# Two gate blocks of each mixer multiplied as a pair, with seven block products in place of eight

## The reference, cut to what matters

```
h = rms_norm(x, pre_g)
proj = h @ w_in            # 2048 x (12*1536 + 3*2048)
# attention q,k,v,z; conv u,b,c,z; retention q,k,v,z; gates g_a, g_c, g_r (2048 columns each)
merged = (sigmoid(g_a) * (o_a @ w_branch_a)
          + sigmoid(g_c) * (o_c @ w_branch_c)
          + sigmoid(g_r) * (o_r @ w_branch_r))
y = merged @ w_out
return x + rms_norm(y, post_g)
```

## Time and profile before

| what | value |
|---|---|
| median of 3 runs (lowest, highest) | 2745.49 us (2745.38, 2746.4) |
| span of the profiled execution | 2743.0 us |
| TensorE matmul busy | 2732.6 us, 12264 instructions |
| DVE busy | 1924.2 us, 2558 instructions |
| ACT busy | 1222.0 us, 1404 instructions |
| 16 DMA engines, share by the loads' queue | 57.4% |

### The profile page before, as it was taken

One profiled execution on the slowest core, in us unless ns is written; L12 is line 12 of the kernel. 1 busy time (PEld: TensorE's weight loads), 2 busy tenths in 40 slices (PEclk: granted clock), 3 DMA queues, 4 the chain that ended last, 5 costly groups with the idle time before them and its releaser, 6 DMA issues.

```text
span 2743.0 us, 30433 instructions
## 1 busy us (share of the span) xinstructions
PE 2732.6 (100%) x12264; PEld 2268.3 (83%) x12264; DVE 1924.2 (70%) x2558; ACT 1222.0 (45%) x1404; POOL 27.5 (1%) x35
## 2 busy tenths in 40 slices
PE   9999999999999999999999999999999999999998
PEld 7888888888888888888878888888888888888887
DVE  6788744777655898858567887457676558977584
ACT  6454544444443334444454545444444433434443
POOL 0000000000000000000000000000000000000000
PEclk9999999999999999999999999999999999999999
DMA  9555566565555555556575555555656565555563
GB/s 333 184 172 196 170 200 194 190 199 188 196 195 190 184 184 176 182 195 221 180 238 175 184 190 179 197 188 187 202 193 198 188 197 177 191 171 182 199 215 138
DMA packets 264732, 529.10 MB, mean 193 GB/s; under 512 B 8464, under 2 KB 8848, under 8 KB 264336
## 3 DMA queue, kind: packets, MB, share of 16 engines
q1 hardware_dynamic: 260976, 517.50, 57.4%
q10 hardware_dynamic: 2608, 4.78, 0.5%
q0 software_dynamic: 1008, 4.87, 0.5%
HBM read 522.94 MB, written 4.19 MB: 192 GB/s over the span
## 4 chain that ended last, share of the span: by engine, by line
PE 99%; DVE 0%; issue 0%; ACT 0%; DVEq 0%; POOL 0%; POOLq 0%
PE ps L651 32%; PE ps L652 32%; PE ps L653 32%; PE ps L586 0%; PE ps L606 0%; PE ps L604 0%; PE ps L603 0%; PE ps L582 0%; PE ps L567 0%; PE ps L587 0%; PE ps L581 0%; PE ps L669 0%; DVE gates L1183 0%; DVE w_trail L913 0%; DVEq L231 0%
## 5 line engine op out<-in xcount | busy, mean ns | idle before, releaser
L913 DVE TENSOR_TENSOR w_trail<-raw,w_lead 128x1024 fp32r<-128x1024 f32 x973 | 1188.7, 1225 | 763.8 <-ACT w_lead L723 754.4
L723 ACT ACTIVATE w_lead<-raw 128x1024 fp32r<-128x1024 f32 x973 | 1028.3, 1060 | 1394.1 <-PE ps L653 1387.3
L651 PE MATMUL ps<-w_lead,hT_lead 128*128 128x512 f32 x3328 | 1299.1, 390 | 0.8 <-issue 0.4
L653 PE MATMUL ps<-w_lead,hT_trail 128*128 128x512 f32 x3328 | 1295.2, 389 | 0.0
L652 PE MATMUL ps<-w_trail,hT_lead 128*128 128x512 f32 x3328 | 1295.1, 389 | 0.0
L651 PEld LDWEIGHTS ps<-w_lead,hT_lead 128*128 128x128 f32 x3328 | 625.0, 188 | 131.1 <-issue 2.2
L653 PEld LDWEIGHTS ps<-w_lead,hT_trail 128*128 128x128 f32 x3328 | 624.9, 188 | 130.0
L652 PEld LDWEIGHTS ps<-w_trail,hT_lead 128*128 128x128 f32 x3328 | 625.1, 188 | 128.4
L651 PE MATMUL ps<-w_lead,oT_lead 128*128 128x512 f32 x576 | 224.3, 389 | 0.0
L653 PE MATMUL ps<-w_lead,oT_trail 128*128 128x512 f32 x576 | 224.1, 389 | 0.0
L652 PE MATMUL ps<-w_trail,oT_lead 128*128 128x512 f32 x576 | 224.1, 389 | 0.0
(11 more groups left out here) (102 smaller groups left out, 781.7 us busy)
## 6 DMA issues: line engine op xcount, KB each, us to landing
raw<-w_in SPq DMA_DIRECT2D x381, 1024.0 KB, 5.1
raw<-w_out SPq DMA_DIRECT2D x32, 1024.0 KB, 5.0
raw<-w_branch_a SPq DMA_DIRECT2D x24, 1024.0 KB, 5.0
raw<-w_branch_c SPq DMA_DIRECT2D x24, 1024.0 KB, 5.0
raw<-w_branch_r SPq DMA_DIRECT2D x24, 1024.0 KB, 5.0
raw<-w_in SPq DMA_DIRECT2D x5, 512.0 KB, 5.0
gates<-x SPq DMA_DIRECT2D x4, 512.0 KB, 13.5
post_gain<-post_norm_g POOLq DMA_DIRECT2D x2, 1024.0 KB, 8.2
```

The source lines that it names most:

```text
L651: pe.matmul(acc, lead[:, k, tok(t)], wl, start=(k == 0), stop=False)
L653: last = pe.matmul(acc, trail[:, k, tok(t)], wl, start=False, stop=(k == BLOCKS[n][2] - 1))
L723: act.activation(w_lead[:, h % SPLIT_SLOTS, :], raw[:, i % RAW_SLOTS, part:part + HALF * COLS], ACT.Copy).then_inc(lead_ready, 1)
L913: dve.tensor_tensor(w_trail[:, s, :], raw[:, i % RAW_SLOTS, part:part + HALF * COLS], w_lead[:, s, :].bitcast(F32), ALU.subtract).then_inc ...
```

## The change

The third and fourth gate blocks of each mixer (j = 2 and 3) become a pair. On the first half of the contraction (tiles 0 to 7, taken as two chunks c = 0 and 1 of four tiles) the eight products of (token tile) x (chunk) x (block) are replaced by seven: p1, q5, p6, p7, q3, p2, q4. Four of them (`SUM_AFTER`: q5, p6, p7, q4) take a sum of two weight chunks, which DVE makes in place in `raw`; four (`FORMS`) take a combination of token-side chunks, made once a layer in `sh_lead` and `sh_trail`. The second half of the contraction is multiplied as before. A product has two units of 6 matmuls each. The pair's units (numbered 0 to 21 in what follows, with H for a unit of 12 matmuls of block n or n+1) stand in this order: p1 p1 H q5 q5 H p6 p6 H p7 p7 H q3 q3 H p2 p2 H q4 q4 H H. Before, the two blocks had 16 units of 12 matmuls.

```diff
-RAW_SLOTS = 4
+RAW_SLOTS = 5
+PAIRED_GATES = {"attention": (2,), "conv": (2,), "retention": (2,)}
...
+PRODUCTS = {"p1": ((0, 0), None), "q5": ((0, 0), (1, 0)), "p6": ((0, 0), (1, 1)), "p7": ((1, 0), (1, 1)),
+            "q3": ((1, 1), None), "p2": ((0, 1), None), "q4": ((0, 0), (0, 1))}
+PAIR_ORDER = ("p1", 0, "q5", 0, "p6", 0, "p7", 0, "q3", 1, "p2", 1, "q4", 1, 1)
+PAIR_CHUNK_ORDER = ((0, 0), (1, 0), (0, 2), (1, 1), (0, 3), (1, 2), (0, 1), (1, 3))
+
+SUM_AFTER = {"q5": "p1", "p6": "q5", "p7": "p6", "q4": "p2"}
...
+STARTS = [0]
+for _kind, _n, _at in UNITS:
+    STARTS.append(STARTS[-1] + (1 if _kind in PRODUCTS else TILES))
...
+    return next(h for h in range(HALVES) if STARTS[h] >= STARTS[FIRST_HALF[n]] + TILES * at)
...
-                out.setdefault(FIRST_HALF[first_block(mixer, g)] + at + offset, []).append((what, mixer, g))
+                out.setdefault(unit_after(first_block(mixer, g), at) + offset, []).append((what, mixer, g))
...
+FORM_STEPS = ("whole", "sums", "lead", "trail")
+FORMS_FROM = 2 * B
+
+PAIR_COPY_DUE = {UNIT_AT[kind, n, 1] + AHEAD: (kind, n) for n in PAIRS for kind in ("p1", "p6", "p7")}
+PAIR_REST_DUE = {UNIT_AT[kind, n, 1] + AHEAD + 1: (kind, n) for n in PAIRS for kind in ("p6", "p7")}
+SUM_DUE = {UNIT_AT[before, n, 1]: (kind, n) for n in PAIRS for kind, before in SUM_AFTER.items()}
...
-        post_gain = sb("post_gain", [P, D_MODEL])
-        v_sb = sb("v_sb", [P, TILES, COLS])
-        q_sb = sb("q_sb", [P, TILES, COLS])
+        vq_sb = sb("vq_sb", [P, 2, TILES, COLS])
+        v_sb, q_sb = vq_sb[:, 0], vq_sb[:, 1]
+        post_gain = vq_sb[:, :, :, :].rearrange("p a t c -> p (a t c)")
...
-        prodT = sb("prodT", [P, HPB, 2 + SEQ])
...
+        prodT = probsT[:, :, 0:2 + SEQ]
...
+            def product(l, h, what, n, part):
...
+                    elif what in ("p6", "p7"):
+                        pe.wait_ge(pair_copied, 2 * pair_no(l, n) + 1 + (what == "p7"))
...
+                pe.wait_ge(*split_done(l, h))
...
+                    pe.matmul(acc[:, :], lead, wl, start=opens, stop=False, skip_group_check=again)
+                    pe.matmul(acc[:, :], lead, wt, start=False, stop=False, skip_group_check=again)
+                    last = pe.matmul(acc[:, :], trail, wl, start=False, stop=closes, skip_group_check=again)
+                last.then_inc(half_done, 1)
...
+                elif what in SUM_AFTER and part == 0:
+                    act.wait_ge(summed, len(SUM_AFTER) * pair_no(l, n) + list(SUM_AFTER).index(what) + 1)
...
+                elif kind == "gate" and n in PAIR_OF:
+                    act.wait_ge(*moved_out(l, n))
+                    for t in range(TILES):
+                        cols = slice(COLS * j, COLS * (j + 1))
+                        act.activation(gates[:, t, cols], gates[:, t, cols], ACT.Sigmoid,
+                                       scale=x_rstd[:, t:t + 1]).then_inc(gate_ready, 1)
...
+                copied = act.activation(dst, side(l, step)[:, :], ACT.Copy)
...
+                dve.wait_ge(*split_done(l, UNIT_AT[SUM_AFTER[what], n, CHUNK // HALF - 1]))
+                dve.wait_ge(*chunk_landed(l, into))
+                dve.wait_ge(*chunk_landed(l, added))
+                dve.tensor_tensor(dst, dst, raw[:, SLOT_OF[l, added][0], :], ALU.add).then_inc(summed, 1)
...
+                rest = dve.tensor_tensor(gates[:, t, COLS * (j + 1):COLS * (j + 2)], side(l, q_step)[:, :],
+                                         gates[:, t, COLS * col:COLS * (col + 1)], ALU.subtract)
...
+                    for t in range(TILES):
+                        dve.tensor_tensor(gates[:, t, cols], bank(n, t)[:, :], gates[:, t, cols],
+                                          ALU.add).then_inc(evicted[n % 2], 1)
...
                     if h < HALVES:
                         split_trail(l, h)
+                    if h in SUM_DUE:
+                        chunk_sum(l, *SUM_DUE[h])
+                    if h in PAIR_REST_DUE:
+                        pair_rest_of(l, *PAIR_REST_DUE[h])
+                    if 0 <= h - FORMS_FROM < len(FORM_STEPS):
+                        form_work(l, FORM_STEPS[h - FORMS_FROM])
```

More of the change, by code:

```diff
@@ L45 @@
 GATES_AT = 12 * GROUPS
-STEPS = {"attention": HPB + HPB // 2,
-         "conv": 0,
-         "retention": HPB + HPB // 2}
 X_STEPS = TILES * KT // HPB
 MERGE_TURNED = 2
-MERGE_STEPS = TILES * (OUT_BLOCKS - MERGE_TURNED)
+PLAIN_TAIL = tuple(("gate", j) for j in range(OUT_BLOCKS)) + tuple(("branch", j) for j in range(OUT_BLOCKS))
+TAIL = {"attention": PLAIN_TAIL, "conv": PLAIN_TAIL, "retention": PLAIN_TAIL}
+PAIRED_GATES = {"attention": (2,), "conv": (2,), "retention": (2,)}
 CONST_PARTS = (("ident", P), ("log_count", 3 * P), ("causal", 3 * P), ("cos", TILES * 64),
@@ L75, in layer_blocks @@
                                ("mix", mixer, role, g)))
[L76 to L79, removed]
+        for kind, j in TAIL[mixer]:
+            if kind == "gate":
+                blocks.append(("w_in", COLS * (GATES_AT + OUT_BLOCKS * b + j), KT, ("gate", mixer, "", j)))
+            else:
+                blocks.append((mixer, COLS * j, KT_MIX, ("branch", mixer, "", j)))
     for j in range(OUT_BLOCKS):
@@ L86, with gate_block, branch_block, first_block @@
 NBLOCKS = len(BLOCKS)
[L87 to L92, removed]
+PER_BLOCK_GROUP = len(ROLES["attention"])
+MIXER_BLOCKS = PER_BLOCK_GROUP * GROUPS + 2 * OUT_BLOCKS
+BLOCK_NO = {b[3]: n for n, b in enumerate(BLOCKS)}
+def gate_block(mixer, j):
+    return BLOCK_NO["gate", mixer, "", j]
+def branch_block(mixer, j):
+    return BLOCK_NO["branch", mixer, "", j]
+def first_block(mixer, g):
+    return MIXER_BLOCKS * MIXERS.index(mixer) + PER_BLOCK_GROUP * g
+PAIRS = [gate_block(m, j) for m in MIXERS for j in PAIRED_GATES[m]]
+PAIR_OF = {n + i: n for n in PAIRS for i in range(2)}
+PRODUCTS = {"p1": ((0, 0), None), "q5": ((0, 0), (1, 0)), "p6": ((0, 0), (1, 1)), "p7": ((1, 0), (1, 1)),
[3 more added lines that the diff above has]
+SUM_AFTER = {"q5": "p1", "p6": "q5", "p7": "p6", "q4": "p2"}
+def layer_units():
+    units, n = [], 0
+    while n < NBLOCKS:
+        if n in PAIRS:
+            at = [2 * CHUNK, 2 * CHUNK]
+            for step in PAIR_ORDER:
+                if step in PRODUCTS:
+                    units += [(step, n, part) for part in range(CHUNK // HALF)]
+                else:
+                    units.append(("half", n + step, at[step]))
+                    at[step] += HALF
+            n += 2
+        else:
+            units += [("half", n, k) for k in range(0, BLOCKS[n][2], HALF)]
+            n += 1
+    return units
+UNITS = layer_units()
+HALVES = len(UNITS)
+def touches(n, unit):
+    kind, m, _at = unit
+    return m == n if kind == "half" else n in (m, m + 1)
+FIRST_HALF = [min(h for h, u in enumerate(UNITS) if touches(n, u)) for n in range(NBLOCKS)] + [HALVES]
+LAST_HALF = [max(h for h, u in enumerate(UNITS) if touches(n, u)) for n in range(NBLOCKS)]
+UNIT_AT = {u: h for h, u in enumerate(UNITS)}
+FIRST_NORMAL = [min(h for h, u in enumerate(UNITS) if u[:2] == ("half", n)) for n in range(NBLOCKS)]
 PAIRED = 2
@@ L118, with layer_chunks @@
-PER_BLOCK_GROUP = len(ROLES["attention"])
-MIXER_BLOCKS = PER_BLOCK_GROUP * GROUPS + 2 * OUT_BLOCKS
+        return UNITS[h]
+    i, part = (h % PAIRED, h // PAIRED) if h < CROSSED else divmod(h, CHUNK // HALF)
+    return "half", i % PAIRED, CHUNK * (i // PAIRED) + HALF * part
+def layer_chunks():
+    chunks, n = [], 0
+    while n < NBLOCKS:
+        if n in PAIRS:
+            chunks += [(n + i, c) for i, c in PAIR_CHUNK_ORDER]
+            n += 2
+        else:
+            chunks += [(n, c) for c in range(BLOCKS[n][2] // CHUNK)]
+            n += 1
+    return chunks
@@ new lines, with chunk_list, chunk_and_part, last_use @@
+CHUNK_LIST = layer_chunks()
+CHUNKS = len(CHUNK_LIST)
+PAIRED_LIST = [(i % PAIRED, i // PAIRED) for i in range(PAIR_CHUNKS)] + CHUNK_LIST[PAIR_CHUNKS:]
+def chunk_list(l):
+    return CHUNK_LIST if l else PAIRED_LIST
+def chunk_and_part(l, h):
+    kind, n, at = place(l, h)
+    if kind == "half":
+        return chunk_list(l).index((n, at // CHUNK)), at % CHUNK // HALF
+    (i, c), _added = PRODUCTS[kind]
+    return CHUNK_LIST.index((n + i, c)), at
+def last_use():
+    uses = {}
+    for l in range(DEPTH):
+        for h in range(HALVES):
+            i, _part = chunk_and_part(l, h)
+            uses[l, i] = h
+            kind, n, at = place(l, h)
+            if kind in PRODUCTS and PRODUCTS[kind][1] is not None and at == 0:
+                i, c = PRODUCTS[kind][1]
+                uses[l, CHUNK_LIST.index((n + i, c))] = h
+    return uses
@@ L123, with raw_slots @@
+LAST_USE = last_use()
+def raw_slots():
+    free_at, held, out = [None] * RAW_SLOTS, [0] * RAW_SLOTS, {}
+    for l in range(DEPTH):
+        for i in range(CHUNKS):
+            s = min(range(RAW_SLOTS), key=lambda s: (free_at[s] is not None, free_at[s] or (0, 0), s))
+            out[l, i] = s, held[s], free_at[s]
```

(6 more changed lines are left out.)

265 lines of the change are left out of this document (193 added, 72 removed).

## The result

The changed kernel takes 2754.39 us (median of 6 runs, 2753.65 to 2756.37) against 2745.78 us before (6 runs of the same sessions); the ratio is 1.0032, with a 95% interval of 1.002 to 1.0043. The forecast was 2749, with a range of 2737 to 2757, made from 2745.5 us before (3 runs). So the change makes the kernel 8.6 us slower, where 3.3 were forecast. The span of the profiled execution grew from 2743.0 to 2752.3 us.

What follows compares the result with a forecast made beforehand. TensorE bounds the kernel, but DVE paces triples with a sum. Saving 16.3 us against stalls of 2 x (8.3 + 1.0 + 0.5) gives +3.3 us: 2745.5 becomes 2749 us, range 2737 to 2757.

Steps and rivals of the forecast that it cites:

- The saving: On TensorE, six pairs drop 72 matmuls at 0.227 us each, saving 16.3 us, 0.6% of the time.
- The sum's price: On DVE, one addition of two 128x2048 weight chunks takes 2.3 us, at least 1.23 and at most 2.45.
- Attention's stall: In attention's pair, DVE's sums and z pieces make TensorE wait before units 4, 5, 7 and 8, together 8.3 us.
- rival B: TensorE's clock falls behind waits in attention's pairs, 2.8 us per slow stretch, 5.5 to 11 us in all; chance 0.14.
- B's nearer case: One slow-clock stretch in each attention pair, 5.5 us in all, giving 2754.5 us.
- Retention: In retention's pair, sums and ACT's two sigmoids, which delay lead 4, make splits late; taken as 1.0 us.
- Conv: In conv's pair, with nothing but splits before it, the same walk along DVE's list gives 0.5 us of stall.
- The forms and the ring: Forms, 7.6 us of DVE and 2.1 of ACT a layer at units 16 to 19, and five-slot `raw`: cost 0.
- the copies of p6 and p7: ACT's waiting copies in attention's pair, some 0.63 us each, end before their product is due.
- A: DVE's idle 30% and the lead of four units hide the sums: 2729, or 2737 with attention's stall halved; chance 0.20.
- C: More DVE stalls in conv and retention, 1 to 2 us in each of six pairs: 2753 to 2758; chance 0.17.
- The tight spot named for the load of chunk (0,1): Load asked for when split 10 is done, due some 6 us later: 0 to 1 us a pair, taken as 0.

## Why the prediction was right, and where it was off

- **The saving.** 72 matmuls at 0.227 us, 16.3 us: right. The run without sums shows it bare, -2.70 to -2.77 us a pair in conv and retention. By the spacing that the Trainium skill gives for bf16 (TensorE: Matmul & The Clock Gate, section "Wait — 56ns, not 53.3ns?", 215.7 ns) a pair would save 2.59 us, an estimate that the trace doesn't bear out.
- **The sum's price.** Taken as 2.3 us from a line through two rows, measured 2.29 (24 times). Two rows can't show that the prices lie on a line; the third point does.
- **Attention's stall.** The walk along DVE's list gave unit 8 at 349.0 in the times of before; it starts at 349.49, of which 0.4 is the start's offset: 8.3 us forecast, 8.3 measured. Step by step, for units 4, 5, 7 and 8, it forecast stalls of 0.6, 3.1, 1.35 and 3.3 us; in the attention pair whose clock stayed up (the run with the added reductions, layer 1) 0.5, 3.1, 1.2 and 3.3 are lost before them. Shown by experiment too: of 10.1 us lost in a pair, 2.1 to 2.5 are left when either the pieces or the sums go.
- **The clock** was priced as rival B and left out of the sum; it happened, in part, and its sign, matmuls 0.43 us apart, was named among those of being wrong. The step that failed is the sum's term for attention, 8.3 us a pair: it costs 8.3 + 1.7. B's own price was 2.8 us for a slow stretch, taken from the start; it is 1.7 here, about eight matmuls, and of the two stretches in a pair only the second is paid. So B gives 3.4 us over the kernel, not 5.5 to 11. That B's nearer case, 2754.5, is the measured time is luck: its 5.5 us stand where 3.4 of the clock and 1.8 of retention belong.
- **Retention** was mis-sized: "I take 1.0 us", measured 1.9. The prediction let the sigmoids delay lead 4, but had no term for lead 3: ACT holds it for the sum, and the sigmoids queue behind it. So unit 5 comes 1.1 us late and not 0.4. The earlier sigmoids give 0.9 back, which shows it.
- **Conv**: 0.5 us forecast, 0.5 to 0.6 measured. The forms and the ring at nothing: right, as the run without pairs shows; the copies of p6 and p7 too, as conv and retention save their full 2.7 us with them in the run without sums.
- **The rivals.** A fell: the slack of four slots does not absorb it. C, more stalls of DVE's kind, is true of retention only, 0.9 us in two pairs, as against 1 to 2 in six.

The sum as it came out: -16.3 + 2 x (8.3 + 1.7 + 1.9 + 0.6) = +8.7 us, where the medians differ by 8.6 (2754.39 - 2745.78) and the marks of the one profiled execution add up to 8.9. The forecast was +3.3: of the gap, 3.4 us are the clock, 1.8 retention. The range held the time, but of the three outcomes that the prediction weighed, slower (0.34) came, and not same (0.44).

The tight spot named for the load of chunk (0,1) did not show in the change, but it did as soon as attention's stalls were gone. That those had given the load its time is my reading; no run tests it.

## What to carry to other kernels

A fast-product scheme saves multiplications and pays in preparation: here each product of half the length needs as much splitting as a full unit, and four of seven need a sum besides. Where TensorE is the bound on average, read the preparing engine's list in the stretch of the change, instruction by instruction against the lead that the buffers give; 70% busy over the whole says nothing about it. Then move what is not urgent out of that stretch: the same pairs with the transposes of z, its two copies and two sigmoids elsewhere turn +0.32% into -0.37%.

## What the runs showed of the hardware that was not expected

- TensorE's clock fell to its lower level behind waits of 2.8 us, and behind waits of 2.1 us in conv's pairs with the added reductions; behind others of 2.84 and 3.01 us it did not. So the length of a wait near 3 us does not settle it, and what does stays open. The Trainium skill, TensorE: Matmul & The Clock Gate, section "Part 1: The HAM clock gate", describes the fall after idleness and the recovery under work. The trace agrees with the recovery, with 0.43 us between some eight matmuls and 0.227 after them, and with the fall behind some of these waits but not all.
- A slow stretch can be free: where the preparing engine sets the next unit, TensorE's slowness fills what would have been a wait (10.12 us from unit 5 to unit 8 with the slow stretch and without it).
- A GpSimd addition of 128x2048 takes 4.5 us where it starts before a split of DVE and 5.5 where it starts behind one, beside DVE's 2.29. Each holds the other off, so here the idle GpSimd was no place for work beside DVE instructions with two operands.
